# Filling the borders of a two-model kernel: output projection, attention input, MLP norm and rotary tables reordered

## The reference

```
first block, two layers; every norm is modulate(x) = rms(x) * g * (1+scale) + shift
  layer 0: gated linear attention over 768 tokens, 4 heads, chunks of 64, both directions;
           y = (rms(o) * silu(r)) @ w_out           x += gate * y
           x += gate * (silu(conv3(h @ Wa)) * (h @ Wv)) @ ffn_out       width 2816
  layer 1: neighbourhood attention, q of the 512 latent tokens, k and v of all 768
           x += gate * y ;  x += gate * conv_ffn(h), latent tokens only
  x = rms(x) * final_g
second block, two layers
  h = rms(x) * g ; latent attention (8 heads), stick-breaking attention (8), retention (8)
  x += (sum over three branches of sigmoid(gate) * (y_n @ w_branch_n)) @ w_out
  h = rms(x) * norm_mlp_g ;  x += relu(h @ w_up)^2 @ w_down            width 4096
out = rms(x) * final_norm_g
```

## Time and profile before

| | |
|---|---|
| runs | 3929.17 us median of 3 (3923.21 to 3929.26) |
| profiled execution | 3926.22 us; span from first to last instruction 3924.4 us |
| mean granted TensorE clock | 0.982 |
| PE, PEld busy | 96%, 79% of the span |
| DVE, ACT, POOL busy | 44%, 38%, 6% |
| DMA | 333.95 MB, mean 85 GB/s |

### The profile page before, as it was taken

One profiled execution on the slowest core, in us unless ns is written; L12 is line 12 of the kernel. 1 busy time (PEld: TensorE's weight loads), 2 busy tenths in 40 slices (PEclk: granted clock), 3 DMA queues, 4 the chain that ended last, 5 costly groups with the idle time before them and its releaser, 6 DMA issues.

```text
span 3924.4 us, 45303 instructions
## 1 busy us (share of the span) xinstructions
PE 3769.1 (96%) x18912; PEld 3081.2 (79%) x18912; DVE 1708.0 (44%) x2614; ACT 1480.9 (38%) x2355; POOL 239.6 (6%) x191
## 2 busy tenths in 40 slices
PE   7998889999998999999989999999999999999998
PEld 6898767888887977788766768878886676887887
DVE  5326735544544136544445443343334444334332
ACT  5245423332323236323345533232324544224232
POOL 0000000000000000000000001120110000112011
PEclk8999989999999999999999999999999999999999
DMA  5330022333321222223311123323221122332332
GB/s 197 104 113 2 17 70 70 108 120 124 111 86 55 89 68 71 85 92 102 100 51 53 60 73 97 105 83 100 95 98 55 44 70 70 100 105 86 97 96 81
DMA packets 108701, 333.95 MB, mean 85 GB/s; under 512 B 11472, under 2 KB 26704, under 8 KB 108368
## 3 DMA queue, kind: packets, MB, share of 16 engines
q1 hardware_dynamic: 108496, 331.06, 26.4%
HBM read 327.35 MB, written 2.10 MB: 84 GB/s over the span
## 4 chain that ended last, share of the span: by engine, by line
PE 91%; DVE 5%; ACT 3%; issue 1%; DMA 1%; POOL 0%; SPq 0%; DVEq 0%; ACTq 0%
PE ps L599 67%; PE ps L635 6%; PE ps L683 2%; PE ps L618 2%; PE ps L644 1%; PE ps L1165 1%; PE ps L992 1%; PE ps L827 1%; PE ps L1013 1%; PE ps L1001 1%; PE ps L854 1%; DMA raw<-weights_d 1%; PE ps L1086 1%; PE ps L1089 1%; PE ps L1108 1%
## 5 line engine op out<-in xcount | busy, mean ns | idle before, releaser
L2067 DVE TENSOR_TENSOR wlo<-raw,whi 128x1024 fp32r<-128x1024 f32 (+3 forms) x643 | 740.7, 1157 | 982.9 <-ACT whi L1326 982.3
L1326 ACT ACTIVATE whi<-raw 128x1024 fp32r<-128x1024 f32 (+3 forms) x643 | 620.9, 977 | 798.0 <-PE ps L599 633.3
L599 PE MATMUL ps<-bh,whi 128*128 128x512 f32 x1248 | 495.4, 397 | 0.1
L599 PE MATMUL ps<-bh,wlo 128*128 128x512 f32 x1248 | 487.3, 390 | 0.8 <-DVE wlo L2067 0.8
L599 PE MATMUL ps<-bl,whi 128*128 128x512 f32 x1248 | 487.0, 390 | 0.0
L599 PE MATMUL ps<-ah,whi 128*128 128x512 f32 (+2 forms) x1424 | 420.2, 354 | 6.9 <-ACT whi L1326 6.9
L599 PE MATMUL ps<-ah,wlo 128*128 128x512 f32 (+2 forms) x1424 | 418.6, 353 | 0.9 <-DVE wlo L2067 0.8
L599 PE MATMUL ps<-al,whi 128*128 128x512 f32 (+2 forms) x1424 | 416.3, 351 | 0.0
L599 PEld LDWEIGHTS ps<-ah,whi 128*128 128x128 f32 x1424 | 245.6, 189 | 44.6 <-ACT whi L1326 8.7
L599 PEld LDWEIGHTS ps<-bh,whi 128*128 128x128 f32 x1248 | 235.0, 188 | 57.4 <-issue 7.1
L599 PEld LDWEIGHTS ps<-bh,wlo 128*128 128x128 f32 x1248 | 234.8, 188 | 51.2 <-DVE wlo L2067 1.6
(11 more groups left out here) (348 smaller groups left out, 6131.7 us busy)
## 6 DMA issues: line engine op xcount, KB each, us to landing
raw<-weights_d SPq DMA_DIRECT2D x543, 512.0 KB, 3.4
raw<-weights_d SPq DMA_DIRECT2D x48, 256.0 KB, 2.6
raw<-weights_d SPq DMA_DIRECT2D x44, 192.0 KB, 2.4
x<-nab_d SPq DMA_DIRECT2D x24, 256.0 KB, 2.7
x<-x_t_d SPq DMA_DIRECT2D x4, 1024.0 KB, 6.0
dt<-rtab_d SPq DMA_DIRECT2D x16, 256.0 KB, 2.9
out_d<-x SPq DMA_DIRECT2D x4, 512.0 KB, 3.1
nvb<-nv SPq DMA_DIRECT2D x6, 256.0 KB, 4.5
```

What stands on the lines that cost most here:

```text
L599: m = e.matmul(p[:, 0:n], tiles(w, i)[:, k, :], xs[:, x0 + k, c0:c0 + n], start=pi == 0 and k == 0 and ti == 0, stop=i == job and k == kt ...
L1326: e.activation(flat(WHI, j), raw(j), ACT.Copy).then_inc(q.did("hi", j))
L2067: e.tensor_tensor(flat(WLO, j), raw(j), flat(WHI, j).bitcast(F32), ALU.subtract).then_inc(q.did("lo", j))
```

## The change

1. **Attention output projection.** PE runs the first two chunks of `gla_w_out` in parts: tiles 0 to 2 of the first, statistics of head 3's first half, tiles 3 to 5, statistics of the second half, tiles 0 to 5 of the second chunk, then tiles 6 and 7 of both. Head 3 gets its own `Os` and squares, the query buffers of even and odd heads are swapped, SP's wait is for head 2's outputs, and ACT and DVE make weight halves between the gates. The projection starts one pair of banks later.
2. **Attention input.** Norm `nl`, the pair, the third chunk's halves and three evacuations, then norm `nc`, in buffers of its own (`NNORM`).
3. **MLP of the second block.** The up-projection takes x * g in place of x * g * r, with r the rsqrt of the token; since relu(r u)^2 = r^2 relu(u)^2, the down-projection's result is multiplied by r^2 = exp(-ln(...)). Each residual tile is scaled and split as soon as it is finished, and the last squares are summed behind the pair.
4. **Order alone.** In `tables()` the slices are spread over all eight output tiles; in the latent attention `m_values` stands ahead of `m_scores` in DVE's program; in `conv_ffn` the third chunk is called before the first evacuation.

```diff
@@ weight_plan
     turn = turns(6, 2)
+    next(turn)
     for ct in range(8):
         S("gla_w_out", (0,), 0, 8, plain(128 * ct), next(turn))
@@ pe_program: new
+        def lin_part(i, V, ready, segs, k0, k1):
+            ps = [PS[b] for b in plan[i][6]]
+            for k in range(k0, k1):
+                ...
+                q.wait_ge(("hi", i), *ready(k))
...
-        for s in range(2):
-            gate(3, s)
-        q.note("end_gla", "pe")
+        ahead = [chunk("gla_w_out") for _ in range(2)]
+        lin_part(ahead[0], Y, y_ready, SEGS, 0, 3)
+        gate(3, 0)
+        lin_part(ahead[0], Y, y_ready, SEGS, 3, 6)
+        gate(3, 1)
+        lin_part(ahead[1], Y, y_ready, SEGS, 0, 6)
+        q.note("end_gla", "pe")
@@ act_program, end of attention
-        for n, s in enumerate((0, 0, 1, 1, 0, 1)):
+        for n, s in enumerate((0, 1, 0, 1, 0, 1)):
             next(gates[s])
-            if n in (0, 1):
+            if n in (1, 3):
                 high_half()
@@ dve_program, end of attention
+        q.wait_ge(("gat", 3, 0, 0), ("gat", 3, 0, 1), ("gyl", 2, 1, 0), ("gyl", 2, 1, 1))
+        low_half()
         gates = [gate(3, s) for s in range(2)]
-        for s in (0, 1, 0, 1):
+        next(gates[0])
+        low_half()
+        for s in (1, 0, 1):
             next(gates[s])
@@ sp_program
-        q.wait_ge(("gom", 3, 1, 1))
+        q.wait_ge(("gom", 2, 1, 1))
         weights(first("na_w_qkv") + LOOK + 8)
@@ act_program, attention input
+        n_norm(0, lambda k: by_column(AH, k))
...
+        pair = [chunk("na_w_qkv", n) for n in range(2)]
+        third = chunk("na_w_qkv")
+        for ct, i in enumerate(pair + [third]):
+            evac_q(i, ct)
+        n_norm(1, lambda k: AH[:, k, 0:TC])
@@ act_program, conv_ffn (the same in dve_program)
                         ia, iv = [chunk("ffn_w_in", m) for m in range(2)]
+                        following = chunk("ffn_w_in")
                         gate_in(ia, n)
@@ act_program, MLP
+            def u_high(k):
+                q.wait_ge(("x", f"out{l}", k, 0))
+                e.activation(BH[:, k, :], lat(X, k), ACT.Copy, scale=col("norm_mlp", 8 * l + k)).then_inc(...)
...
-            for _ in norm_high(f"u{l}", f"out{l}", 0, 8, lambda k: BH[:, k, :], UNORM, f):
-                pass
+            pair = [chunk("w_up_2", n) for n in range(2)]
+            third = chunk("w_up_2")
+            for jj, i in enumerate(pair):
+                evac_u(i, jj, 0)
+            ln_exp()
+            q.wait_ge(("sqmm", f"out{l}", 7, 0), ("small",), *f)
+            e.activation(URS, PS[6], ACT.Ln, scale=1.0 / D, bias=col("eps")).then_inc(...)
+            q.wait_ge(("ln", f"out{l}", 0))
+            e.activation(URS, URS, ACT.Exp, scale=-1.0).then_inc(q.did("urs", l))
@@ dve_program, MLP
+            def u_low(k):
+                q.wait_ge(("nh", f"u{l}", k))
+                e.scalar_tensor_tensor(BL[:, k, :], lat(X, k), col("norm_mlp", 8 * l + k), BH[:, k, :].bitcast(F32), ...)
...
             for ct in range(8):
                 add_x(f"out{l}", ct, chunk("w_out_2"))
+                if ct:
+                    u_low(ct - 1)
+            u_low(7)
...
+            def add_down(S, ct, i, n):
+                x, t = lat(X, ct), UTMP[n % 2]
+                q.wait_ge(("mm", i), ("urs", l), *([("x", *added[n - 2], 0)] if n >= 2 else []))
+                e.tensor_tensor(t, PS[plan[i][6][0]], URS, ALU.mult).then_inc(q.did("ev", i, 0))
+                q.wait_ge(("ev", i, 0))
+                e.tensor_tensor(x, x, t, ALU.add).then_inc(q.did("x", S, ct, 0))
@@ pe_program, MLP
                             lin_pair(["w_up_2", "w_up_2"], B, ur, ONE)
+                            stats_add(f"out{l}", 7, 7)
@@ tables(), ACT
             for n in range(2):
-                yield
+                for _ in range(4 - 2 * n):
+                    yield
@@ tables(), DVE: a yield ahead of the wait for the positions, behind the angle, and behind the reduction
+            yield
             q.wait_ge(("pos",))
...
                 yield
-                yield
+                if n == 0:
+                    yield
@@ dve_program, latent attention
+                if n >= 4:
+                    m_values(n - 4)
                 if n < 16:
                     m_scores(n)
-                if n >= 4:
-                    m_values(n - 4)
```

More of the change, by code:

```diff
@@ L452, in build @@
     NP = ring("np", 8, oX0 + 16 * KB)
+    NNORM = [(ring(f"nnrs{b}_", 1, oX0 + (16 + 8 * b) * KB), ring(f"nntr{b}_", 3, oX0 + (18 + 8 * b) * KB)) for b in range(2)]
     NK = at("nk", [128, 8, T0], F32, oX0 + 32 * KB)
@@ L601, in lin @@
                                          skip_group_check=True)
+                m.then_inc(q.did("mm", i))
+        def lin_part(i, V, ready, segs, k0, k1):
+            ps = [PS[b] for b in plan[i][6]]
+            for k in range(k0, k1):
+                if k == 0:
+                    for si, b in enumerate(plan[i][6]):
+                        bank(b, ("ev", i, si))
+                q.wait_ge(("hi", i), *ready(k))
+                for ti, (w, xs) in enumerate(((WHI, V.hi), (WHI, V.lo), (WLO, V.hi))):
+                    if ti == 2:
+                        q.wait_ge(("lo", i))
+                    for p, (c0, n) in zip(ps, segs):
+                        m = e.matmul(p[:, 0:n], tiles(w, i)[:, k, :], xs[:, k, c0:c0 + n],
+                                     start=k == 0 and ti == 0, stop=k == 7 and ti == 2, skip_group_check=True)
+            if k1 == 8:
                 m.then_inc(q.did("mm", i))
@@ L666, in with_stats @@
                     stats_add(S, ct - 1, None, ctx)
-            stats_add(S, 7, 7, ctx)
+            if last:
+                stats_add(S, 7, 7, ctx)
         def ada_chunk(i, cg, g):
@@ L1288, in pe_program @@
                     q.note(f"end_tail{l}", "pe")
-            with_stats(f"out{l}", lambda ct: lin("w_out_2", M, lambda k: [("ml", l, k)], ONE))
+            with_stats(f"out{l}", lambda ct: lin("w_out_2", M, lambda k: [("ml", l, k)], ONE), last=False)
             q.note(f"end_out{l}", "pe")
@@ L1399, in with_stats @@
                     stats_square(S, ct - 1, 7, srcs(ct - 1))
+            if high:
+                high(7)
             stats_square(S, 7, 7, srcs(7))
@@ L1693, in act_program @@
         pair = [chunk("na_w_qkv", n) for n in range(2)]
-        for ct, i in enumerate(pair):
+        third = chunk("na_w_qkv")
+        for ct, i in enumerate(pair + [third]):
             evac_q(i, ct)
-        for ct in range(2, 8):
+        n_norm(1, lambda k: AH[:, k, 0:TC])
+        q.note("end_nnorm", "act")
+        fn = fence("end_nnorm")
+        for ct in range(3, 8):
             evac_q(chunk("na_w_qkv"), ct)
@@ new lines, in act_program @@
+            third = chunk("w_up_2")
[3 more added lines that the diff above has]
+            q.wait_ge(("sqmm", f"out{l}", 7, 0), ("small",), *f)
+            e.activation(URS, PS[6], ACT.Ln, scale=1.0 / D, bias=col("eps")).then_inc(q.did("ln", f"out{l}", 0))
+            q.wait_ge(("ln", f"out{l}", 0))
+            e.activation(URS, URS, ACT.Exp, scale=-1.0).then_inc(q.did("urs", l))
+            for half in range(2):
+                for jj in range(0 if half else 2, 16):
+                    evac_u(third if (half, jj) == (0, 2) else chunk("w_up_2"), jj, half)
@@ new lines, in add_down @@
+            def add_down(S, ct, i, n):
[4 more added lines that the diff above has]
+                e.tensor_tensor(x, x, t, ALU.add).then_inc(q.did("x", S, ct, 0))
+                added.append((S, ct))
+            added = []
+            for n in range(2):
+                chunk("w_up_2", n)
@@ L2786, in dve_program @@
+            chunk("w_up_2")
+            for jj in range(2):
+                evac_u(jj, 0)
+            for half in range(2):
+                for jj in range(0 if half else 2, 16):
+                    if (half, jj) != (0, 2):
+                        chunk("w_up_2")
+                    evac_u(jj, half)
                 for ct in range(8):
                     chunk("w_down_2")
-                    add_x(f"mlp{l}" if half else f"mlph{l}", ct, chunk("w_down_2"))
+                    add_down(f"mlp{l}" if half else f"mlph{l}", ct, chunk("w_down_2"), 8 * half + ct)
```

146 lines of the change are left out of this document (75 added, 71 removed).

## The result

The changed kernel took 3877.10, 3878.59 and 3886.17 us, the kernel before beside it 3928.86 (median): ratio of these runs 0.9881, 95% interval 0.9865 to 0.9898. It is faster by 1.2%. Timed once more in the experiments, the kernel gave 3877.67 (e8, ratio 0.9871, 0.9856 to 0.9886). The median of the other seven executions is 3878.6. The profiled one took 3886.17 us, the longest of the seven, with a span of 3884.4 and a mean granted clock of 0.985.

What follows compares the result with a forecast made beforehand. TensorE, busy 96% of 3924.4 us, was taken as the bound, so only its idle and half-clock time could go. 15.3 + 9.0 + 14.0 - 2.2 + 7.8 + 0.7 = 44.6 us off gave 3885 us, own range 3879 to 3892.

Steps and rivals of the forecast that it cites:

- Linear attention, 15.3 predicted: Border to the output projection: 35.05 us before, 19.7 after, by earlier fetch, early low half and fillers; bounds 9 to 16.
- Neighbourhood attention, 9.0: Input projection: third chunk follows the latent pair, so the fourth starts at 1270.9, not 1279.99; 9.0 us gained, low end 5.
- the feared lateness: Neighbourhood attention: sixth chunk's halves done at 1282.2, wanted at 1281.9 and 1282.3, no cover left; up to 4 us late.
- MLP norm, 14.0: Second block, twice: 7.7 us gained at the projection's border less 0.7 behind the down-projection; bounds 10 and 16.
- Tables, a loss of 2.2: Second feed-forward: 5.8 us gained inside, 6.4 lost in the tail behind it, 1.6 to slow clock; bounds -6 and +1.
- all sixteen passes slow: Square sum behind the second feed-forward: every pass at half clock, 13.6 us; the tables part loses 5.3 instead of 2.2.
- Remainder ahead of scores, 7.8: Latent attention: TensorE's six waits for VectorE's remainder go, 6 x 1.3 = 7.8 us gained.
- the low end of 3: Latent attention: only 3 us gained if the softmax of the tile before comes last instead.
- rival 3: Fewer gaps bring fewer slow-clock stretches, seen in the second latent attention: 3879 us, chance 0.11.
- Third feed-forward chunk, 0.7: Converted early: TensorE's 0.7 us stall, twice, against two conversions delaying the convolution; 0.7 us gained in all (0 to 1.4).
- Rival 1: Covers too thin: attention fillers partly at half clock, sixth chunk's halves late; one 3890 us, both 3895; chance 0.16.
- Rivals 4 to 6: Half the MLP and border gains stay, 3903 (0.04); doubled add paces down-projection, 3952 (0.02); change doesn't take, 3899 (0.02).

Runs made afterwards that it cites:

- e5: Changed kernel with all edits of the border from linear attention to its output projection undone (buffers, partial projection, orders, fetch): 3890.54 us, ratio 0.9909.
- e12: Changed kernel with the fetch of the following weights tied to head 3's outputs again; fillers, orders and buffers stay changed: 3876.85 us, ratio 0.9862.
- e11: Changed kernel without fillers: both statistics of head 3 ahead of the first projection chunk, early fetch kept: 3877.60 us, ratio 0.9871.
- e6: Changed kernel with the context norm again ahead of the evacuation of the first chunks of the neighbourhood attention's projection: 3890.32 us, ratio 0.9902.
- e7: Changed kernel with the second block's MLP norm again ahead of the up-projection, in both layers: 3891.69 us, ratio 0.9911.
- e1: Changed kernel with the rotary tables made as in the kernel before: 3875.11 us, ratio 0.9866.
- e3: Changed kernel with VectorE's table pieces merged, so the second angle and the sines come one output tile earlier: 3870.28 us, ratio 0.9854.
- e2: Changed kernel with VectorE's remainder behind the score operations again in the latent attention: 3888.00 us, ratio 0.9898.
- e10: e3 with the remainder behind the score operations again in the latent attention: 3886.83 us, ratio 0.9892.
- e9: e3 with ScalarE's copies of the turned weights also put ahead of the exponentials in the latent attention: 3869.09 us, ratio 0.9845.

## Why the prediction was right, step by step

The forecast was 3885 us, a gain of 44.6; the medians are 3878.6 over the seven executions (3882.4 on record) and 3877.7 for e8 alone. The stages of the table give 43.6, the whole trace 40.0, and the medians 50, since the profiled execution was the longest of the seven. That the total came out so close is in part luck, as the latent attention below shows. Stage by stage:

- *Linear attention, 15.3 predicted:* 15.0, and 15.0 when undone (e5). The mechanism was named too narrowly. The prediction put the fetch and the fillers first; e12 and e11 show them worth at most 0.4 and some 1.2 us, each alone; both together were not undone. By subtraction the gain lies in what e11 and e12 share, and there are three such things: the low half of the first chunk made ahead of the gates; the statistics' work on ScalarE no longer behind the conversion of a chunk just being fetched; and six k-steps of the second chunk ahead of those of the first that need head 3. The last covers time too: in the changed kernel the first chunk's six k-steps and the statistics are through at 527.05, and head 3's last remainder is made at 532.2. I didn't separate these three.
- *Neighbourhood attention, 9.0:* 8.8, and 7.8 when undone (e6). The context norm ended well ahead of its deadline; the feared lateness didn't come.
- *MLP norm, 14.0:* 7.7 and 7.5 at the borders, less 0.8 and 0.7: 13.6, and 13.6 when undone (e7).
- *Tables, a loss of 2.2:* a loss of 1.5 to 4.1 (e1). The gain side, 5.8, came as said (57.5 to 51.7), though the two terms named for it, 3.89 and 1.7, add to 5.6. The tail's terms read 2.5 + 2.1 + 0.5 + 1.3, predicted 2.6 + 2.0 + 0.6 + 1.7. The 1.7 for GpSimd's add was a mean over two kinds: in the kernel before, its adds took 1.3 us where VectorE was busy for 0.4 us of them or less, and 1.8 where it was busy for 0.66 or more. GpSimd is waited for 7.54 us instead of 1.55, so 6.0 later where 6.4 was said. The slow clock cost more than the 1.6 taken: 1.8 in the four passes right behind the wait, which I had left out, and 1.05 in the stretch of the sixteen of the next sum (9.99 us against 8.93 in the earlier trace rows). That makes 8.8 of the 8.85 in the table, against 8.0. The case for which the clock gate rule of the Trainium skill ("TensorE: Matmul & The Clock Gate", Part 1: The HAM clock gate) was cited, all sixteen passes slow, would have taken 13.6 us and didn't come: the first six distances between them are 0.84 us or more and the others 0.43 to 0.53 (in the kernel before it is the first three). The lower clock thus ended while the passes ran, which agrees with what that page says of activity. Nor did a table load stand in the tail. Where one does stand in the changed kernel's chain, with its next operation ready, it costs 1.3 us from the end of the operation ahead to the start of the next:

```profile
1231.52 0.43 ACT sq L1420
...
1231.98 1.26 ACT L1381
...
1233.25 0.70 ACT nnrs L1393
```

The 2.66 us for a switch in the Trainium skill ("ScalarE: Activation LUTs", What ACT_TABLE_LOAD costs) is twice that; here the measurement decides. The longer wait of the tail could be avoided altogether (e3).
- *Remainder ahead of scores, 7.8:* this step failed as put: "Now it runs while the scores are still being multiplied. Gain 6 x 1.3 = 7.8". The remainder does, but TensorE then waits for the copy behind the softmax exponentials, as the low end of 3 had it; TensorE's waits there are 9.4 us in e2 and 7.0 in the changed kernel, 2.4 less over both layers, where 7.8 was said. In the profiled pair the first layer even gained nothing. The part is still worth more than 2.4: less slow clock fell in these stages, and the means of 89.05 and 85.3 give 3.7 a layer. So its worth, 7.5 by the stages and 9 to 17 by the medians of e2 and e10, is about the predicted size or above, for a reason that stood in rival 3. That the term came out near its size is luck. Why this order meets less slow clock is not shown (e10).
- *Third feed-forward chunk, 0.7:* TensorE's two idle pieces (0.48 and 0.53 us before) are gone; but the first one's stage is only 0.4 shorter in the trace after and 0.2 in e8, less than the clock moves there. The part wasn't tested alone.

Rival 3 (fewer slow stretches, 3879) is what the seven executions with their median of 3878.6 look like, and it was given 0.11; the 3885 itself lies at the upper end of them (3876.0 to 3886.2). The forecast counted gaps and left the clock that they bring in this stage to a rival; the earlier trace rows had shown it, 0.77 against 1.00. Rival 1's thin covers: no slack was missed, and with the clock at 1.00 in the fillers nothing ran late. Rivals 4 to 6 didn't occur. The only wait for a high half that is longer than before (3.0 us against 1.3) stands at 84 us, where the change touches nothing, and is 1.3 again in e8.

## What to carry to other kernels

When one wait of an in-order engine is removed, follow the next releaser's own queue too: what stands there ahead of the instruction that TensorE will need next can take the place of the old wait (here 7.0 us of the 9.4). Price an idle piece not only by its length but by the clock behind it, over several executions, since one pair of profiles showed a gain of 0 in one layer and 7 us in the other for the same edit. A side computation cut into slices must have its last slice end before the stage's last tile; if it moves, place it from the end, not from the start.

## What was not expected of the hardware

The same instructions of the first latent attention took 87.72 us in one execution and 84.61 in another, with 6.8 us of slow clock in the one and none in the other. With one order changed this happened in 4 of 18 stages against 5 of 6, though the idle time of a stage differs by only 1.1 us. Slow clock began behind idle pieces as short as 0.82 us, in a stage where TensorE is otherwise busy. The place of slow clock in one stage also moved between executions of one program, so that a kernel's own runs spread over 10 us (e8, e11) or over 1.1 (e9). The granted clock of each execution goes with its time (e10: 0.987 at 3878.4 us and 0.984 at the three from 3886.4 to 3888.7; e9: 0.987 to 0.988 for all four), so the spread goes with slow clock too; why it falls in some executions and not in others, one profile of each can't tell.
